# The opening in two parts of the feature columns: modulation pieces multiplied by TensorE directly, constants of its own ahead of them

## The chip, the cores and the metric

One core of one Trainium2 chip runs the whole program in one launch. The metric is the device time of the program in microseconds (us); lower is better. KB are 1,024 bytes, as in the profile.

## The reference, cut to what matters

Four layers act on one sequence of 512 tokens with 1,024 features. Each layer first needs its modulation: a vector of 1,024 conditions times a 1,024 x 3,072 matrix, split into shift, scale and gate. The first layer starts with

```python
cond = jax.nn.silu(c)
mod = cond @ ada_w[l] + ada_b[l]
shift, scale, gate = jnp.split(mod, 3, axis=-1)
h = x * (1.0 + scale[:, None, :]) + shift[:, None, :]
proj = h @ w_in
u, v, z_a, x_b, z_b = jnp.split(proj, ...)
v = layer_norm(v, norm_g, norm_b)          # per head of 256 features
sv = W_s (masked) applied to v over blocks of 128 positions, + b
a = u * sv * silu(z_a)
```

Nothing of `proj` can start before shift and scale of at least one block of 128 features are known, and for these all 1,024 rows of those matrix columns must have been read. Everything is float32 in and out.

## The kernel before, in words

The features lie across the partitions in eight blocks of 128 (`DC` = 8); `x`, `h_hi` and `h_lo` hold them as 8 x 512 tokens. For a product of full precision each operand is split into a high and a low part (`w_hi`, `w_lo`, `h_hi`, `h_lo`) and `mm3` issues three matmuls (lines 971 to 973). ScalarE makes the high parts, VectorE the low ones (`split_tile`, lines 1557 and 1883; `h_low`, line 2173, from ScalarE's `h_hi` and GpSimd's `tmp`, line 2637). Weights come as tiles of 128 x 2,048 (1,024 KB) in two turns of buffers: tile T uses the buffers of tile T - 2, so its split waits for the products of that tile.

`plan_steps` (line 88) writes out one list of steps that all engines walk through. It begins with `first_mods` and `h`, then tiles 0 to 3 (kind V, one head of 256 features each, two chunks of 256 tokens), tiles 4 to 7 (kind U), and so on. At the step `tile` T ScalarE and VectorE split tile T + 1, and VectorE sums two modulation pieces of later layers (`ada_pieces`, lines 1917 and 1925). `spatial_rows` and `spatial(h)` are TensorE's products over positions (lines 1379 and 1390) into banks 4 and 5; VectorE takes their results to `park` (line 2381). Before the change `spatial(h - 1)` stands behind the two chunks of head h. The chunks alternate between banks 0 and 1, and the first tile alone is done as a pair, block by block (`chunk_pair`, line 990), so that it can follow the blocks of `h` as they appear.

In the opening SyncE issues, in this order: the columns of constants `cols` (98.5 KB), weight tile 0, sixteen modulation pieces `ada_first` of 128 rows x 1,024 columns (512 KB each; eight of the shift, eight of the scale) with the constants `mats` and `rmats_raw` (288 and 256 KB) behind the first, then `x` in four transfers of 512 KB, weight tile 1, `ws` and `bs`. VectorE multiplies each piece by its column of `cond` and adds it to `acc` (`ada_piece`, line 1892), except pieces 1 and 3 (`DIRECT_PIECES`), which TensorE multiplies as eight one-column products each (line 1219). TensorE then sums `acc` over the partitions with a column of ones (lines 1224 and 1236), with fillers of 512 columns between (`keep_busy`, line 978), and VectorE makes `h_shift` and `h_scale` (lines 2192 and 2196). The last piece is summed in two halves, so that four blocks of the scale come out ahead.

```python
pe.wait_ge(masks_done, 1)
pe.wait_ge(upper_done, 1)
keep_busy(22)
```

Of the kernel before, what the change touches and what calls it, by code (L numbers as in the profile page):

```python
# [25 lines left out]
P = 128  # L26
D = 1024
# [48 lines left out]
DIRECT_PIECES = (1, 3)  # L76
# [11 lines left out]
def plan_steps():  # L88
# [8 lines left out]
    def begin(late_ada=False, late_low=False):  # L97

        T = st["T"]
        st["T"] += 1  # L100
        steps.append(dict(op="tile", T=T, late_ada=late_ada, late_low=late_low))
        return T
# [285 lines left out]
def build(nc, wt, adat, colst, matst, rmatst, xt, pos, wst, bst, poolt, decayt, rot, out):  # L388
# [11 lines left out]
    with ExitStack() as ctx:  # L400
# [186 lines left out]
        w_hi_done = sem("w_hi_done")  # L587
        w_lo_done = sem("w_lo_done")
# [3 lines left out]
        ada_first_landed = [sem(f"ada_first_landed{i}") for i in range(16)]  # L592
# [16 lines left out]
        ada_half = sem("ada_half")  # L609
# [129 lines left out]
        def pieces_summed(q):  # L739

            return q - sum(i < q for i in DIRECT_PIECES)
# [6 lines left out]
        for q in range(2 * SEC, SEC * UNITS):  # L748
            ada_in[q] = 16 * len(piece_at[q][0]) + ada_in.get(q - 2, 0)

# [80 lines left out]
        PAIRED = {d["C"] for d in kinds if (d["kind"], d.get("h"), d.get("c")) == ("V", 0, 0)}  # L831
# [65 lines left out]
        def _(sp):  # L897
            sp.dma_start(cols[:], colst).then_inc(cols_in, 16)
            sp.dma_start(w_raw[0][:], wt[0]).then_inc(w_landed[0], 16)
            for i in range(2 * SEC):  # L900
                sp.dma_start(ada_first[:, i, :], adat[i]).then_inc(ada_first_landed[i], 16)
# [3 lines left out]
            for i in range(4):  # L905
                sp.dma_start(x[:, 2 * i:2 * i + 2, :], xt[:, 2 * i:2 * i + 2, :]).then_inc(x_landed[i], 16)
            sp.dma_start(w_raw[1][:], wt[1]).then_inc(w_landed[1], 16)
# [31 lines left out]
            for T in range(NT):  # L939
# [8 lines left out]
                if T == 4:  # L948

                    sp.wait_ge(ada_done, pieces_summed(2 * SEC))  # L950
# [17 lines left out]
        def _(pe):  # L968
# [6 lines left out]
            def keep_busy(n):  # L975

                for i in range(n):
                    pe.matmul(bank[:, 3, :], upper, rmats[:].rearrange("p a b -> p (a b)"), start=True, stop=True)  # L978
# [11 lines left out]
            def chunk_pair(d):  # L990

                T, C = d["T"], d["C"]
                for c in range(2):
                    wait_taken(pe, BEFORE_IN_BANK[C + c])
                for k in range(DC):
                    wait_h(layer[0], k)
                    for c in range(2):
                        dst = bank[:, (C + c) % 2, :]
# [142 lines left out]
            def chunk(d, late=False, early=False):  # L1141
# [6 lines left out]
                if C in PAIRED:  # L1148
                    return chunk_pair(d)
                if C - 1 in PAIRED or kind in ("OUT2", "OUT3") and d["n"] < 2:  # L1150
# [62 lines left out]
            def first_mods():  # L1213

                pe.wait_ge(cond_done, 1)
                for i in DIRECT_PIECES:
                    pe.wait_ge(ada_first_landed[i], 16)
                    for j in range(DC):
                        pe.matmul(bank[:, 6, j:j + 1], ada_first[:, i, j * P:(j + 1) * P], cond[:, i:i + 1],
                                  start=i == DIRECT_PIECES[0] and j == 0, stop=False, skip_group_check=True)  # L1220
                pe.wait_ge(const_in, 16)
                pe.wait_ge(ada_done, pieces_summed(SEC))
                for j in range(DC):
                    ins = pe.matmul(bank[:, 6, j:j + 1], acc[:, 0, j * P:(j + 1) * P], ones[:, 0:1],
                                    start=False, stop=True, skip_group_check=True)
                ins.then_inc(first_full, 1)
                pe.wait_ge(masks_done, 1)
                pe.wait_ge(upper_done, 1)
                keep_busy(22)
                for half, bk in ((0, 7), (1, 4)):  # L1230
                    if half == 0:
                        pe.wait_ge(ada_half, 1)
                    else:
                        pe.wait_ge(ada_done, pieces_summed(2 * SEC))
                    for j in range(4 * half, 4 * half + 4):
                        ins = pe.matmul(bank[:, bk, j:j + 1], acc[:, 1, j * P:(j + 1) * P], ones[:, 0:1],
                                        start=True, stop=True)
                    ins.then_inc(first_full, 1)
                keep_busy(4)
# [119 lines left out]
            for d in steps:  # L1359
                op = d["op"]  # L1360
                if op == "tile":
                    pe.wait_ge(w_lo_done, d["T"] + 1)
# [9 lines left out]
                elif op == "first_mods":  # L1372
                    first_mods()
# [1424 lines left out]
```

## Time and profile before

| | |
|---|---|
| time, median of 3 runs | 1318.17 us (1317.94 to 1319.11) |
| time of the profiled execution | 1319.02 us |
| its span, first to last instruction | 1317.2 us |
| TensorE (PE) busy | 1289.7 us, 98% |
| VectorE (DVE) busy | 941.3 us, 71% |
| ScalarE (ACT) busy | 580.2 us, 44% |
| GpSimd (POOL) busy | 357.4 us, 27% |
| transferred | 155.18 MB, mean 118 GB/s |

The span is what the profiler sees of one execution; 1.8 us of the time lie outside it. Busy shares are averages over the whole span: the opening, where this change acts, is its first 3%. PE are matmuls, PEld weight loads, SPq SyncE's queue of transfers. Matmuls are pipelined, so the length of a single one is longer than the distance between two. A float32 matmul appears as two records, each with its own weight load. Times in the rows count from the start of the span.

### The profile page before, as it was taken

The page shows a single profiled execution, that of the slowest core. Times are in us where ns is not written, and L with a number is a line of the kernel's source. Part 1 is how long each engine was busy: PE and PEld are TensorE (multiplying, and loading weights), DVE is VectorE, ACT ScalarE, POOL GpSimd, SP SyncE. Part 2 cuts the span into 40 slices and gives each one's busy share as a digit, 9 for nine tenths or more (in the row PEclk, how much of TensorE's full clock was granted, in tenths as well). Part 3 has the DMA queues.
Part 4 walks back from the last instruction along what each step waited for, and adds up shares of the span by engine and source line. Part 5 has one row for each costly group of instructions (what it writes and reads, how often), then busy time and mean ns, then how long its engine had stood idle before and what let it go on. Part 6 is the DMA issues. An engine that isn't in the chain of part 4 may idle for free.

```text
span 1317.2 us, 18039 instructions
## 1 busy us (share of the span) xinstructions
PE 1289.7 (98%) x6874; PEld 1106.0 (84%) x6874; DVE 941.3 (71%) x1415; ACT 580.2 (44%) x889; POOL 357.4 (27%) x262
## 2 busy tenths in 40 slices
PE   5999999999999999999999999999999999999997
PEld 5998888778898888888888878888888988888887
DVE  7765654796777558888678888776785577776663
ACT  1422322321264347666422587653452477734441
POOL 1200210055620004655434221122115322221122
PEclk9999999999999999999999999999999999999999
DMA  9565666537725620111234311213533111212111
GB/s 376 171 199 180 187 201 193 158 117 204 234 79 153 174 87 21 41 52 51 88 122 142 112 65 64 96 53 110 154 97 115 65 64 65 95 55 75 64 64 64
DMA packets 35093, 155.18 MB, mean 118 GB/s; under 512 B 6848, under 2 KB 9024, under 8 KB 23744
## 3 DMA queue, kind: packets, MB, share of 16 engines
q1 hardware_dynamic: 35008, 154.04, 36.9%
q8 instruction: 54, 0.88, 0.3%
q14 instruction: 31, 0.25, 0.1%
HBM read 151.92 MB, written 2.10 MB: 117 GB/s over the span
## 4 chain that ended last, share of the span: by engine, by line
PE 88%; DVE 5%; issue 3%; ACT 1%; POOL 1%; DMA 1%; SPq 0%; DVEq 0%; POOLq 0%; ACTq 0%
PE bank L971 25%; PE bank L973 24%; PE bank L972 24%; PE bank L1334 2%; PE bank L1319 1%; PE bank L1338 1%; PE bank L1179 1%; DVE keep L2477 1%; PE bank L1510 1%; PE bank L1537 1%; PE bank L1535 1%; DMA ada_first<-adat 1%; PE bank L1307 1%; PE bank L1306 1%; PE bank L978 1%
## 5 line engine op out<-in xcount | busy, mean ns | idle before, releaser
L971 PE MATMUL bank<-h_lo,w_hi 128*128 128x512 f32 (+1 forms) x1064 | 407.1, 383 | 0.7 <-DVE k_both L2045 0.5
L973 PE MATMUL bank<-h_hi,w_hi 128*128 128x512 f32 (+1 forms) x1064 | 402.5, 378 | 0.0
L972 PE MATMUL bank<-h_hi,w_lo 128*128 128x512 f32 (+1 forms) x1064 | 402.2, 378 | 0.0
L1883 DVE TENSOR_TENSOR w_lo<-w_raw,w_hi 128x2048 fp32r<-128x2048 f32 (+2 forms) x91 | 207.1, 2275 | 75.6 <-ACT w_hi L1557 75.4
L971 PEld LDWEIGHTS bank<-h_lo,w_hi 128*128 128x128 f32 x1064 | 200.2, 188 | 37.6 <-issue 1.8
L973 PEld LDWEIGHTS bank<-h_hi,w_hi 128*128 128x128 f32 x1064 | 200.1, 188 | 37.7
L972 PEld LDWEIGHTS bank<-h_hi,w_lo 128*128 128x128 f32 x1064 | 200.3, 188 | 36.3 <-issue 0.2
L1557 ACT ACTIVATE w_hi<-w_raw 128x2048 fp32r<-128x2048 f32 (+2 forms) x91 | 166.7, 1832 | 89.7 <-PE bank L973 72.9
L1925 DVE SCALAR_TENSOR_TENSOR acc<-ada_raw,cond_four,acc 128x1024 f32<-128x1024 f32 x62 | 87.5, 1411 | 3.9 <-DMA ada_raw<-adat 1.0
L1685 ACT ACTIVATE tmp<-bank 128x512 f32<-128x512 f32 x48 | 28.8, 600 | 112.3 <-PE bank L973 111.1
L2477 DVE TENSOR_TENSOR_SCAN keep<-keep,rmats 128x127 f32<-128x127 f32 (+2 forms) x64 | 57.8, 942 | 1.0
L2599 POOL TENSOR_TENSOR beta<-beta,mats 128x256 f32<-128x256 f32 (+1 forms) x40 | 41.4, 1058 | 58.6 <-ACT beta L1842 58.6
L971 PE MATMUL bank<-mixc_lo,w_hi 128*128 128x512 f32 (+1 forms) x144 | 53.7, 373 | 0.0
L973 PE MATMUL bank<-mixc_hi,w_hi 128*128 128x512 f32 (+1 forms) x144 | 52.6, 365 | 0.0
L972 PE MATMUL bank<-mixc_hi,w_lo 128*128 128x512 f32 (+1 forms) x144 | 52.6, 365 | 0.0
L2578 POOL TENSOR_TENSOR sum<-sum,sqr 128x512 f32<-128x512 f32 x22 | 47.9, 2178 | 1.7
L2678 POOL TENSOR_TENSOR rope_t<-qr_f,sin 32x512 f32<-32x512 f32 x28 | 38.0, 1358 | 31.2 <-ACT qr_f L1814 28.8
L2565 POOL TENSOR_SCALAR mixa_hi<-park 128x512 fp32r<-128x512 f32 x8 | 11.9, 1491 | 124.4 <-DVE park L1999 124.4
L2565 POOL TENSOR_SCALAR mixc_hi<-sz 128x512 fp32r<-128x512 f32 x16 | 23.8, 1490 | 68.8 <-DVE sz L2292 68.8
L2624 POOL TENSOR_TENSOR mixf<-o_sum,ag 128x512 f32<-128x512 f32 x8 | 10.4, 1299 | 114.6 <-DVE o_sum L2532 114.6
L2577 POOL TENSOR_TENSOR sqr<-x 128x512 f32<-128x512 f32 x22 | 34.5, 1569 | 14.3 <-DVE x L2036 13.1
L2565 POOL TENSOR_SCALAR mixb_hi<-park 128x512 fp32r<-128x512 f32 x6 | 12.0, 2026 | 92.9 <-PE bank L973 92.9
(359 smaller groups left out, 2688.1 us busy)
## 6 DMA issues: line engine op xcount, KB each, us to landing
w_raw<-wt SPq DMA_DIRECT2D x83, 1024.0 KB, 5.5
ada_raw<-adat SPq DMA_DIRECT2D x256, 128.0 KB, 2.9
ada_first<-adat SPq DMA_DIRECT2D x16, 512.0 KB, 12.2
ada_raw<-adat SPq DMA_DIRECT2D x32, 256.0 KB, 5.7
w_raw<-wt SPq DMA_DIRECT2D x8, 640.0 KB, 3.9
spare_raw<-wt SPq DMA_DIRECT2D x3, 1024.0 KB, 5.1
x<-xt SPq DMA_DIRECT2D x4, 512.0 KB, 15.5
out<-outf SPq DMA_DIRECT2D x16, 128.0 KB, 1.8
```

The lines of the kernel that those rows point to most:

```text
L971: pe.matmul(dst, ah, bl, start=start, stop=False, skip_group_check=True)
L972: pe.matmul(dst, al, bh, start=False, stop=False, skip_group_check=True)
L973: return pe.matmul(dst, ah, bh, start=False, stop=stop, skip_group_check=True)
L1557: act.activation(w_hi[wb[T]][:, 0:n], w_raw[wb[T]][:, 0:n], ACT.Copy).then_inc(w_hi_done, 1)
L1883: dve.tensor_tensor(w_lo[wb[T]][:, 0:n], w_raw[wb[T]][:, 0:n], f(w_hi[wb[T]][:, 0:n]), ALU.subtract).then_inc(w_lo_done, 1)
L1925: dve.scalar_tensor_tensor(acc[:, g % 2, :], src, c, acc[:, g % 2, :], ALU.mult, ALU.add).then_inc(ada_done, 1)
L2477: ins = dve.tensor_tensor_scan(k, k, floor, 1.0, ALU.mult, ALU.max)
L2565: return pool.tensor_scalar(dst, src, 1.0, None, ALU.mult)
L2577: link(pool.tensor_tensor(sqr[:], x[:, n, :], x[:, n, :], ALU.mult))
L2578: ins = pool.tensor_tensor(sum2[:], sum2[:], sqr[:], ALU.add)
L2599: pool.tensor_tensor(blocks, blocks, strict.unsqueeze(1).broadcast_to([P, len(at), P]), ALU.mult).then_inc(seen_done, 1)
L2678: pool.tensor_tensor(rope_t[to, :], qr_f[of, :], sin1[of, :], ALU.mult).then_inc(qr_turned, 1)
```

## The change

The matrix columns of the opening are loaded and used in two parts: part 0 is feature blocks 0 to 4 (640 columns), part 1 blocks 5 to 7 (384 columns). Weight tiles 0 and 1 are loaded and split in the same parts. Modulation pieces come two in a transfer. In part 0, shift and scale, and in part 1 of the shift, every second piece (1, 3, 5, 7) is multiplied by TensorE directly; in part 1 of the scale VectorE sums all eight. TensorE starts with ten products of 197 columns of `cols`, as soon as these have landed, and puts one such product (shift) or two fillers (scale) behind each direct piece. After part 0 it works through blocks 0 to 4 of tiles 0 and 1 (`first_blocks`), with the direct pieces and sums of part 1 in between, then through blocks 5 to 7 of both. Tiles 0 and 1 so need four banks: the V chunks use banks 0 to 3. The splits of tiles 3 and 4 and the `spatial` steps move later in the list; `spatial(0)` stands behind tile 2, `spatial(1)` behind tile 3, `spatial(2)` and `spatial(3)` in tiles 4 and 5.

```diff
-DIRECT_PIECES = (1, 3)
+DIRECT_PIECES = {(0, 0): (1, 3, 5, 7), (0, 1): (1, 3, 5, 7), (1, 0): (1, 3, 5, 7), (1, 1): ()}
+FIRST_BLOCKS = 5
+X_PARTS = ((0, 2), (2, 4), (4, 5), (5, 8))
...
-    steps.append(dict(op="h", l=0))
-
-    for h in range(GH):
-        T = begin()
-        chunk("V", T, h=h, c=0)
-        chunk("V", T, h=h, c=1)
-        if h == 0:
-            steps.append(dict(op="spatial_rows"))
-        else:
-            steps.append(dict(op="spatial", h=h - 1))
-        after_tile(T)
+    steps.append(dict(op="h", l=0, part=0))
+    steps.append(dict(op="first_blocks"))
+    steps.append(dict(op="h", l=0, part=1))
+    both = [begin(split=False), begin()]
+    head_pair(0, both[0])
+    split_ahead(3)
+    steps.append(dict(op="spatial_rows"))
+    head_pair(1, both[1])
+    T = begin(split=False)
+    chunk("V", T, h=2, c=0)
+    split_ahead(4)
+    chunk("V", T, h=2, c=1)
+    spatial(0)
+    after_tile(T)
+    T = begin(split=False)
+    head_pair(3, T)
+    spatial(1)
+    after_tile(T)
...
-            if kind == "U" and i == 0:
-                steps.insert(len(steps) - 1, dict(op="spatial", h=GH - 1))
+                if kind == "U" and (i, sub) in ((0, 1), (1, 0)):
+                    spatial(2 + i)
...
+            elif d["kind"] == "V":
+                bk = 2 * (d["h"] % 2) + d["c"]
...
+            weights(0, 0)
+            for i in range(SEC):
+                ada_pair(i, 0)
                 if i == 0:
                     sp.dma_start(mats[:], matst).then_inc(const_in, 16)
                     sp.dma_start(rmats_raw[:], rmatst).then_inc(rmats_in, 16)
...
+            for i in range(3):
+                features(i)
+            weights(1, 0)
+            for i in range(SEC // 2):
+                ada_pair(i, 1)
+            weights(0, 1)
+            features(3)
+            for i in range(SEC // 2, SEC):
+                ada_pair(i, 1)
+            weights(1, 1)
...
             def first_mods():
 
+                pe.wait_ge(cols_in, 16)
+                warm_up(10)
                 pe.wait_ge(cond_done, 1)
...
+                for u in range(2):
+                    for k in DIRECT_PIECES[0, u]:
+                        direct_piece(0, u, k)
+                        if u == 1 and k == 1:
+                            pe.wait_ge(masks_done, 1)
+                            pe.wait_ge(upper_done, 1)
+                        if u == 1:
+                            keep_busy(2, 3)
+                        else:
+                            warm_up(1)
+                    if u == 0:
+                        pe.wait_ge(const_in, 16)
+                    first_sums(0, u, 6 + u)
+                keep_busy(5, 3)
+
+            def warm_up(n):
+
+                for i in range(n):
+                    pe.matmul(bank[:, 3, 0:NCOL], cols[:, 0:P], cols[:], start=True, stop=True)
+
+            def direct_piece(part, u, k):
+
+                pe.wait_ge(ada_first_landed[(SEC * u + k) // 2][part], 16)
+                for j in FIRST_K[part]:
+                    pe.matmul(bank[:, 6 + u, j:j + 1], ada_first[:, SEC * u + k, j * P:(j + 1) * P], cond[:, k:k + 1],
+                              start=k == 1 and j == FIRST_K[part][0], stop=False, skip_group_check=True)
...
+            def first_blocks():
+
+                pe.wait_ge(first_lo, 1)
+                chunk_pair(PAIRED[0], FIRST_K[0])
+                pe.wait_ge(first_lo, 2)
+                for k in FIRST_K[0]:
+                    chunk_pair(PAIRED[1], (k,))
+                    for i in DIRECT_PIECES[1, 0][2 * k:2 * k + 2]:
+                        direct_piece(1, 0, i)
+                    if k == FIRST_BLOCKS - 3:
+                        first_sums(1, 0, 6)
+                    if k == FIRST_BLOCKS - 2:
+                        first_sums(1, 1, 7)
+                keep_busy(4, 5)
...
+                elif op == "h" and d["part"] == 0:
+                    first_columns(0)
+                    for k in FIRST_K[0]:
+                        h_low(k)
+                        if 1 <= k < FIRST_BLOCKS:
+                            first_piece(left + k - 1)
+                elif op == "first_blocks":
+                    split_first(1, 0, first_hi, first_lo)
+                    for i in range(left + FIRST_BLOCKS - 1, right):
+                        first_piece(i)
+                    split_first(0, 1, w_hi_done, w_lo_done)
+                    for i in range(right, len(FIRST_ORDER)):
+                        first_piece(i)
+                    first_columns(1)
+                elif op == "h" and d["part"] == 1:
+                    for k in FIRST_K[1]:
+                        h_low(k)
+                    split_first(1, 1, w_hi_done, w_lo_done)
```

`first_piece` (VectorE) is the old sum on one part's columns; `first_sums` is the old column sum over the part's blocks; `first_columns(part)` makes `h_shift` and `h_scale` of the part's blocks. On ScalarE the step `first_blocks` splits the first part of tile 1 and the second of tile 0, and the second part of tile 1 follows part 1 of `h`.

## Rows read from the trace of the kernel before

**Rows 1.** The page: TensorE's busy time, and the chain by engine.

```profile
PE 1289.7 (98%) x6874; PEld 1106.0 (84%) x6874; DVE 941.3 (71%) x1415; ACT 580.2 (44%) x889; POOL 357.4 (27%) x262
...
PE 88%; DVE 5%; issue 3%; ACT 1%; POOL 1%; DMA 1%; SPq 0%; DVEq 0%; POOLq 0%; ACTq 0%
```

**Rows 2.** Chain that ended last, opening: start us, us, what.

```profile
4.84 9.73 DMA ada_first<-adat
...
18.76 1.29 DVE acc L1925
...
20.19 3.55 PE bank L1224 x16
23.74 7.56 PE bank L978 x22
31.30 1.68 PE bank L1236 x16
32.98 1.02 PE bank L978 x4
34.00 0.10 issue
34.10 0.36 PE bank L971
```

**Rows 3.** Windows, TensorE alone: us, busy (records), granted clock, DMA share, GB/s.

```profile
34.10:45.70 11.60, 11.60 (x97) 1.00 0.42 167
```

**Rows 4.** Windows, all engines: PE, PEld, DVE, ACT, POOL, then as above.

```profile
10.00:20.00 10.00, 6.96 (x32) 6.90 (x32) 8.21 (x8) 0.00 (x0) 1.91 (x2) 1.00 1.03 410
20.00:30.00 10.00, 9.81 (x33) 8.49 (x34) 9.10 (x10) 0.00 (x0) 0.00 (x0) 1.00 1.03 410
```

**Rows 5.** Timeline of VectorE: start us, us, instruction, idle before and releaser.

```profile
14.60 5.45 DVE L1925 SCALAR_TENSOR_TENSOR acc<-ada_first,cond,acc 128x1024 f32<-128x1024 f32 x4 [1.28 <-DMA ada_first<-adat]
...
20.99 8.23 DVE L1925 SCALAR_TENSOR_TENSOR acc<-ada_first,cond,acc 128x1024 f32<-128x1024 f32 x6 [0.28 <-DMA ada_first<-adat]
29.32 1.41 DVE L1921 SCALAR_TENSOR_TENSOR acc<-ada_first,cond,acc 128x512 f32<-128x512 f32 x2
...
32.12 0.16 DVE L2196 SCALAR_TENSOR_TENSOR h_scale<-bank,cols 128x4 f32<-128x4 f32 x1 [1.31 <-PE bank L1236]
...
33.26 0.69 DVE L2173 TENSOR_TENSOR h_lo<-tmp,h_hi 128x512 fp32r<-128x512 f32 x1
34.53 0.69 DVE L2173 TENSOR_TENSOR h_lo<-tmp,h_hi 128x512 fp32r<-128x512 f32 x1 [0.58 <-POOL tmp L2637]
...
43.47 2.28 DVE L1883 TENSOR_TENSOR w_lo<-w_raw,w_hi 128x2048 fp32r<-128x2048 f32 x1
...
48.45 0.75 DVE L1981 BATCH_NORM_STATS2 v_stats<-tmp 128x6 f32<-128x256 f32 x2
...
50.70 2.16 DVE L2371 SCALAR_TENSOR_TENSOR rb<-bank,cols,bs 128x128 f32<-128x128 f32 x8
```

**Rows 6.** Timeline of ScalarE and GpSimd, in the same columns.

```profile
6.74 1.91 ACT L1557 ACTIVATE w_hi<-w_raw 128x2048 fp32r<-128x2048 f32 x1 [3.83 <-DMA w_raw<-wt]
...
8.85 2.44 POOL L2585 TENSOR_TENSOR rmats<-mats 128x128 fp32r<-128x128 f32 x1 [8.42 <-DMA mats<-matst]
9.46 0.52 ACT L1691 ACTIVATE rmats<-rmats_raw 128x384 fp32r<-128x384 f32 x1 [0.81 <-DMA rmats_raw<-rmatst]
```

**Rows 7.** Timeline of TensorE, 10 to 18 us.

```profile
10.86 6.96 PE L1219 MATMUL bank<-cond,ada_first 128*128 128x1 f32 x32 [10.86 <-DMA ada_first<-adat]
```

**Rows 8.** Windows of line 978 alone: us, PE, PEld, granted clock, DMA.

```profile
23.60:26.40 2.80, 2.80 (x7) 2.22 (x8) 1.00 1.02 407
...
29.20:31.20 2.00, 2.00 (x10) 1.40 (x8) 1.00 1.02 408
```

**Rows 9.** Chain that ended last, around the first spatial products.

```profile
58.22 1.79 PE bank L1390 x16
```

**Rows 10.** DMA issues: operands, count, KB each, us from issue to landing.

```profile
w_raw<-wt SPq DMA_DIRECT2D x83, 1024.0 KB, 5.5
...
w_raw<-wt SPq DMA_DIRECT2D x8, 640.0 KB, 3.9
```

More of the change, by code:

```diff
@@ L749, in build, with first_summed @@
             ada_in[q] = 16 * len(piece_at[q][0]) + ada_in.get(q - 2, 0)
+        FIRST_COLS = (slice(0, FIRST_BLOCKS * P), slice(FIRST_BLOCKS * P, D))
+        FIRST_WEIGHTS = (slice(0, FIRST_BLOCKS * HD), slice(FIRST_BLOCKS * HD, TILE))
+        FIRST_K = (range(FIRST_BLOCKS), range(FIRST_BLOCKS, DC))
+        FIRST_ORDER = [(part, u, k) for part in range(2) for u in range(2) for k in range(SEC)
+                       if k not in DIRECT_PIECES[part, u]]
+        def first_summed(part, u):
+            return sum((p, v) <= (part, u) for p, v, k in FIRST_ORDER)
         def wait_tile_done(eng, T):
@@ L898, in _, with weights, ada_pair, features @@
             sp.dma_start(cols[:], colst).then_inc(cols_in, 16)
-            sp.dma_start(w_raw[0][:], wt[0]).then_inc(w_landed[0], 16)
-            for i in range(2 * SEC):
-                sp.dma_start(ada_first[:, i, :], adat[i]).then_inc(ada_first_landed[i], 16)
+            def weights(T, part):
+                c = FIRST_WEIGHTS[part]
+                sp.dma_start(w_raw[T][:, c], wt[T, :, c]).then_inc((w_landed if part else first_landed)[T], 16)
+            def ada_pair(i, part):
+                c = FIRST_COLS[part]
+                i2 = slice(2 * i, 2 * i + 2)
+                sp.dma_start(ada_first[:, i2, c],
+                             adat[i2, :, c].rearrange("i p d -> p i d")).then_inc(ada_first_landed[i][part], 16)
+            def features(i):
+                k = slice(*X_PARTS[i])
+                sp.dma_start(x[:, k, :], xt[:, k, :]).then_inc(x_landed[i], 16)
+            weights(0, 0)
+            for i in range(SEC):
+                ada_pair(i, 0)
                 if i == 0:
@@ L1147, in chunk @@
                     return
-                if C in PAIRED:
-                    return chunk_pair(d)
-                if C - 1 in PAIRED or kind in ("OUT2", "OUT3") and d["n"] < 2:
+                if C == PAIRED[0]["C"]:
+                    for pair in PAIRED:
+                        pe.wait_ge(w_lo_done, pair["T"] + 1)
+                        chunk_pair(pair, FIRST_K[1])
+                if C in IN_PAIRS or kind in ("OUT2", "OUT3") and d["n"] < 2:
                     return
@@ new lines, in first_sums @@
+            def first_sums(part, u, bk):
+                pe.wait_ge(first_sum, first_summed(part, u))
+                own = not DIRECT_PIECES[part, u]
+                for j in FIRST_K[part]:
+                    ins = pe.matmul(bank[:, bk, j:j + 1], acc[:, u, j * P:(j + 1) * P], ones[:, 0:1],
+                                    start=own and j == FIRST_K[part][0], stop=True, skip_group_check=True)
+                ins.then_inc(first_full, 1)
+            def first_blocks():
[11 more added lines that the diff above has]
+                keep_busy(4, 5)
@@ L1696, in _ @@
                 if op == "tile":
-                    for T in split_with(d["T"]):
+                    for T in split_with(d["T"]) if d["split"] else ():
                         split_tile(T)
+                elif op == "split_ahead":
+                    split_tile(d["T"])
+                elif op == "first_blocks":
+                    split_first(1, 0, first_hi)
+                    split_first(0, 1, w_hi_done)
                 elif op == "chunk":
@@ L2347, in _ @@
                     T = d["T"]
-                    if not d["late_low"]:
+                    if d["split"] and not d["late_low"]:
                         for t in split_with(T):
```

155 lines of the change are left out of this document (75 added, 80 removed).

## The prediction, made before the change was built

> **What bounds the kernel now.** I read the page first. TensorE is busy for 98% of the span and carries 88% of the chain that ended last [rows 1]. So what happens in the first 34 us decides this change, and whatever TensorE wins there lasts only if it does not wait longer later.
>
> The chain of the opening came next [rows 2]. The reader is to see four links: a transfer of `ada_first` that lands at 14.57, VectorE's sums, TensorE's column products and fillers, and at 34.10 the first product of the layer. Before 34.10 TensorE does no product of the layer. From 34.10 to 45.70 it runs one tile of V (96 products of 256 columns) without a gap [rows 3], 0.12 us each, 1.45 us for the twelve of one feature block.
>
> Then the transfers. The two windows from 10 to 30 us move 410 GB/s at a DMA share of 1.03 [rows 4]: the queue is full. Counting what was issued in order, 4,226 KB had to land by 14.57 and 6,786 KB by 20.97 (VectorE waits for pieces 4 and 9) [rows 5]: 2,560 KB in 6.4 us, 2.5 us for 1,000 KB. That line gives t = 4.0 + KB x 0.0025. It also hits the first weight tile (1,122 KB: 6.8, seen 6.74), `mats` (1,922 KB: 8.8, seen 8.85) and `rmats_raw` (2,178 KB: 9.4, seen 9.46) [rows 6]. The last piece (9,858 KB) is due at 28.6. VectorE, at 1.37 us a piece, starts it at 29.3 [rows 5]: transfers and VectorE are both nearly the bound, and 5.5 us follow from 28.6 to 34.10.
>
> **The change, part by part.** (1) *Part 0 of the columns.* Five of eight blocks are 640 columns. Ahead of them lie 98.5 + 640 (first weights) + 544 (constants) KB, then eight pairs of 640 KB, 1.6 us each. By the line the pairs land at 7.4, 10.4, 12.0, 13.6, 15.2, 16.8, 18.4 and 20.0; the constants lie between the first two. 3,456 KB of the old load are simply behind: 8.6 us. SyncE's issues, 0.4 to 0.7 us each, are fewer and not the limit. Rows become 2,560 bytes; `mats` and `rmats_raw` have rows of 2,304 and 2,048 bytes and kept the line, so I charge nothing here; 1,536-byte rows of part 1 have no row.
>
> (2) *VectorE's sums* shrink from 14 pieces of 1,024 to 8 of 640 columns. An update costs 1.28 us for 1,024 and 0.70 for 512 [rows 5]; between them 0.85 for 640. One per 1.6 us pair: VectorE is done at 20.0 + 0.1 + 0.85 = 20.95 and is no bound.
>
> (3) *TensorE's direct pieces* take the rest. One column with 128x128 weights is two records. At the lower clock 32 of them took 6.96 us, 0.435 us a product; the 8 products of the later sums took 1.68 us, 0.21 [rows 2, 7]. The filler between tells the clock: 7 in 2.8 us up to 26.4 (0.40 to 0.43 for 512 columns, that is 1.2 GHz), 10 in 2.0 us after 29.2 (0.21, 2.4 GHz) [rows 8]; the column of granted clock reads 1.00 in both. So 7 us of one-column work did not lift it and 5.5 us of wide work did, and 1.7 us of one-column work after did not drop it. The new `warm_up(10)` is ten 197-column products. The spatial products, 128 columns in the same type, take 1.79/8 = 0.22 us [rows 9], so a 197-column one is 0.34, and 0.69 at half clock: ten from 2.8 us last until 6.3 to 9.7. I take the rise at about the time seen, done at 8.0 to 8.5. After that a pair costs 5 x 0.21 + 0.34 = 1.4 us in the shift and 1.05 + 0.44 = 1.5 in the scale, under the 1.6 of a pair. But the five shift sums (1.05) go between: pair 3 done 15.0, sums 16.0, then 17.5, 19.0, 20.5, 22.0, and the scale sums 23.05. TensorE ends 3 us behind the last landing and is the new bound of the opening.
>
> (4) *From the sums to the first product.* Now the first four scale columns are out at 31.98 (31.14 plus four products), `h_scale` starts at 32.12, `h_lo` at 33.26, TensorE at 34.10 [rows 2, 5]: 2.1 us. The features are on time (block pairs at 21.3 and 22.6). First product at 25.2 instead of 34.1: **8.9 us earlier**.
>
> (5) *Supply of blocks 0 to 4.* `h_lo` comes every 1.27 us [rows 5] against a need of 1.45. Four part-1 updates (0.56 us, extrapolated to 384 columns) now stand behind blocks 1 to 4 on VectorE, and their pairs land at 25.7, 26.7, 27.7 and 28.6. Each block then costs 0.69 + 0.56 and lands for TensorE by 30.2, needed at 31.0. Next `w_lo` of tile 1's first part: ScalarE is free at 27.0, weights landed 24.8, VectorE 30.8 to 32.25; TensorE asks at 25.2 + 7.2 = 32.4. The margin is 0.2 us, and what is late on VectorE is late there.
>
> (6) *Added to TensorE's real stretch*: 12 direct products and 6 sums at 0.21 = 3.8 us, `keep_busy(4, 5)` 0.9 (hides the step below): **4.7 us back**. Tile 1's part ends 32.4 + 7.2 + 3.8 = 43.4, fillers 44.3. The scale sums stand before the last block at 41.3; their last pair lands at 35.3 and VectorE's eight updates end by 38. `first_full` 4 at 41.95, plus 2.0 gives block 5 at 44.0: hidden by the fillers and one block; without them the wait would be the same time. Then 3 + 3 blocks end both tiles at 52.9, and the row sums (0.9) at 53.8. Before, the same work ends at 58.2 [rows 9]. **Gain so far 4.4 us.**
>
> (7) *What queues up behind.* Splits of tiles 2 to 4 and the four V posts now come in a lump. Tile 2 waits for tile 0's end at 48.6: ScalarE 1.9 and VectorE 2.3 us (1.91 and 2.28 seen [rows 5, 6]) give 52.9, needed 53.8. From there VectorE is behind: a V post takes 2.25 us and `rb` 2.2 [rows 5]. Two posts 57.4, tile 3's `w_lo` waits for ScalarE's root, then 61.2, `rb` 63.4, two posts 68.1, two pieces 70.3, V(2,0) 72.5, tile 4's `w_lo` 76.1, V(2,1) 78.4, `spatial(0)`'s two results 79.1 and 79.8. `spatial(1)` on TensorE now stands after tile 3, at 78.6, and needs those banks back: **0.55 us lost**. Tiles 3, 4 and 5 ask at 67.1, 80.9 and 93.7, margins 6, 5 and 3 us. On SyncE the load of tile 3 now waits for `w_lo` of tile 1's second part, at 48.1 instead of 45.75 [rows 5]; it lands some 5.5 us later [rows 10], at 53.6, and ScalarE, held by its roots, does not come to it before 57. Behind it stand the piece loads and the `poolw` load, which wait for VectorE's first updates of group 2, as they do now; tile 5's weights, behind those, land near 78 and are split from 86 on. If this cover were absent, each microsecond of VectorE past 79 would be one of TensorE.
>
> Sum: 8.9 - 4.7 + 0.2 (the old stretch from 34.1 to 58.2 holds 0.2 us of change-overs that 0.12 us a product does not count, and I count none in the new one) - 0.55 = 3.85 us. The profiled execution took 1319.02 (span 1317.2 and 1.8 around it); less 3.85 is 1315.2. The median is 0.85 under that execution, so **1314.3**. A no-change band is 0.2%, 2.6 us.
>
> **A rule against it.** The Trainium skill, DMA: Bandwidth & Descriptors, section Measured (under Bandwidth), says to batch transfers to at least 1 MiB for 75% of peak or more, measured there with GpSimd's queue; the change cuts 1,024 KB to 640 and 384. The rows speak against it: 256 KB and 288 KB transfers in the full queue cost only their bytes [rows 4, 6].
>
> **Rivals.** *A. The clock falls again while pairs are awaited* (ends slower). Only 0.34 to 0.44 us of a 1.6 us pair is wide work, and the row shows that one-column work alone never lifted it [rows 7]. Then a shift pair costs 2.2 + 0.69 = 2.9 and a scale pair 3.05: from 9.5 the sums end at 9.5 + 11.6 + 2.2 + 12.2 + 2.2 = 37.7, first product 39.8, and about 2.7 us more until the clock rises: 5.7 + 2.7 + 4.7 = 13 later, 1331. If only the shift half is slow, the scale half from 23.3 ends at 30.4, first product 32.5: 1.6 - 4.7 - 0.5 = 3.6 later, 1322. The gain is gone when TensorE's sums end after about 27. For it: those duties; against: no idle stretch over 1.3 us. Chance 0.16.
>
> *B. The lump costs more.* GpSimd's `tmp` sets the 1.27 us period, and with VectorE fuller it may be 1.6; `w_lo` of tile 1 misses by 1 us, and `spatial(1)` waits 1 more. Gain 1.2 to 2.6: 1315.6 to 1317. Chance 0.19.
>
> *C. The queue loses rate with small transfers.* One 640 KB load alone takes 3.9 us, against 5.5 for 1,024 KB [rows 10]: 0.71 of the time for 0.62 of the bytes, an excess that overlap hides today. If it did not, 6,402 KB would take 15% more, 2.4 us; TensorE's lag absorbs none. Gain 1.4, 1316.8. At three quarters of the rate the last pair lands 5.3 us later and the gain is gone: 1319.6. That is also what the rule of the Trainium skill's page, DMA: Bandwidth & Descriptors, would make of it. Chance 0.04 in all.
>
> *D. As worked out*, 1312.6 to 1315.6 (the direct pieces may run closer to the landings, up to 1 us more gain; tile 1's margin may cost 1). Chance 0.61.
>
> **Numbers.** The low end allows TensorE to be 1 us behind the landings instead of 3: 1312.0. The high end takes in B, C and the milder half of A: 1320.5; above lies about 0.12. Faster: D and a little of B, 0.62. Same: most of B and C, 0.20. Slower: A and a rest, 0.18.
>
> **What would show it.** One-column records at 0.105 us spacing from about 10 us on (A: 0.217); VectorE's last part-0 update ending near 21; first product of 256 columns near 25.2; no gap before tile 1's first product near 32.4; first product of block 5 near 44.3; tile 2's first near 53.8; a wait of about half a microsecond before `spatial(1)`. The prediction fails if the clock drops, or if TensorE waits for `w_lo` or `h_lo` by microseconds between 25 and 80.

## The result, and the profile after

The changed kernel takes 1329.20 us (median of 6 runs, 1328.46 to 1330.92) against 1318.78 for the kernel before (6 runs, 1317.94 to 1320.94): a ratio of 1.008, 95% interval 1.0067 to 1.0093. It is 10.4 us slower, where 1314.3 and faster was forecast. The profiled execution took 1328.74, its span 1326.9. (One of the 19 executions of the kernel before that were run beside x1_vector to x4_bare was in a slow state, 4592.67 us, and counts in no ratio.)

Page of the changed kernel, the lines of the clock and of the chain by engine (40 slices of 33 us):

```profile
PEclk6899999999999999999999999999999999999998
...
PE 88%; DVE 5%; issue 3%; ACT 1%; POOL 1%; DMA 1%; SPq 0%; DVEq 0%; POOLq 0%; ACTq 0%
```

The chain is shared out as before [rows 1]. The clock is not: the first slice has 6 tenths and the second 8. From the third on both kernels read 9, but for the last, 8 instead of 9. Windows of TensorE in the changed kernel (us, busy with records, granted clock, DMA share, GB/s):

```profile
9.30:10.90 1.60, 0.31 (x2) 1.00 1.04 414
12.00:12.60 0.60, 0.60 (x5) 1.00 1.03 393
12.60:13.00 0.40, 0.40 (x3) 0.71 1.04 397
13.00:14.00 1.00, 1.00 (x6) 0.50 1.05 402
39.00:40.00 1.00, 1.00 (x7) 0.50 0.05 20
40.00:41.00 1.00, 1.00 (x10) 0.96 0.00 0
```

The clock fell at about 12.8 us, from 2.4 to 1.2 GHz, and came back at 40.1. Ahead of the fall TensorE had waited 1.4 us for the second pair, and then done five one-column products and one of 197 columns. The chain of the same stretch, with what the low clock did to it:

```profile
10.99 1.28 PE bank L1302 x10
...
20.45 2.13 PE bank L1302 x10
22.58 1.06 PE bank L1038 x2
...
32.61 1.93 PE bank L1310 x10
34.53 2.34 PE bank L1038 x5
36.87 0.23 PE bank L1031
...
46.97 1.23 PE bank L1302 x12
...
66.56 0.86 PE bank L1470 x2
78.92 1.79 PE bank L1481 x16
92.22 1.79 PE bank L1481 x16
```

Line 1302 are the direct products, 1310 the one-column sums, 1038 the fillers, 1031 the first of a block's products, 1470 the row sums, 1481 `spatial`. Five direct products (ten records) take 2.13 us where 1.05 was forecast, two fillers 1.06 instead of 0.44. The group at 10.99, ahead of the fall, took 1.28. The sums end at 34.5 and the first product starts at 36.87 (34.10 before [rows 2]); the chain lets a product start where the one ahead ends, and the timeline, from which the table below is taken, has 36.67.

VectorE in the changed kernel, its timeline:

```profile
10.97 0.89 DVE L2012 SCALAR_TENSOR_TENSOR acc<-ada_first,cond,acc 128x640 f32<-128x640 f32 x1 [1.48 <-DMA ada_first<-adat]
12.63 0.89 DVE L2012 SCALAR_TENSOR_TENSOR acc<-ada_first,cond,acc 128x640 f32<-128x640 f32 x1 [0.78 <-DMA ada_first<-adat]
...
20.91 0.88 DVE L2012 SCALAR_TENSOR_TENSOR acc<-ada_first,cond,acc 128x640 f32<-128x640 f32 x1 [0.77 <-DMA ada_first<-adat]
21.71 0.16 DVE L2304 TENSOR_TENSOR h_shift<-bank,cols 128x5 f32<-128x5 f32 x1
34.57 0.17 DVE L2306 SCALAR_TENSOR_TENSOR h_scale<-bank,cols 128x5 f32<-128x5 f32 x1 [12.70 <-PE bank L1310]
35.71 0.69 DVE L2283 TENSOR_TENSOR h_lo<-tmp,h_hi 128x512 fp32r<-128x512 f32 x1 [0.98 <-POOL tmp L2764]
```

This is the plainest picture of the loss: the last pair is there at 20.9 and VectorE's last update ends at 21.8, but `h_scale` waits 12.7 us for TensorE. Before, the same wait was 1.3 us [rows 5]. The transfers kept nearly their rate: pairs of 640 KB came every 1.66 us, 396 GB/s, against 410 [rows 4].

**Where the 9.2 us up to tile 2 went.** Tile 2's first product starts at 67.42 (66.56 + 0.86); before it is 58.2 without its spatial step [rows 9]. Of this the first product is 2.8 later (36.87 for 34.10, by the chain). The stretch from there to tile 2 takes 30.55 instead of 24.1 us: 1.45 for 16 products at half rate, 3.6 for the 18 one-column products (two groups of 1.23, two of 0.56), 0.93 for the fillers ahead of block 5, and 0.5 that is mostly the slower first product behind each change of type. The spans differ by 9.7. The starts of VectorE's `w_lo` show where the other half microsecond lies: they differ by 9.2 us at 465 us of the kernel before (473.88 for 464.65), by 9.45 at 651 (660.69 for 651.24) and at 1286 (1295.37 for 1285.90), and a last quarter comes behind that. Its cause is not known.

### The profile page after: what moved, and what is told of

Read it like the earlier page. It is cut to its first block, busy times and chain, and to the rows that moved or that the text cites. A ratio compares the mean times of both kernels' runs of the same rounds, so it can differ in the third digit from the quotient of the medians.

```text
span 1326.9 us, 18239 instructions
## 1 busy us (share of the span) xinstructions
PE 1308.4 (99%) x6965; PEld 1123.8 (85%) x6965; DVE 939.6 (71%) x1423; ACT 580.0 (44%) x891; POOL 356.1 (27%) x262
## 4 chain that ended last, share of the span: by engine, by line
PE 88%; DVE 5%; issue 3%; ACT 1%; POOL 1%; DMA 1%; SPq 0%; DVEq 0%; POOLq 0%; ACTq 0%
PE bank L1031 25%; PE bank L1033 24%; PE bank L1032 24%; PE bank L1422 2%; PE bank L1407 1%; PE bank L1302 1%; PE bank L1426 1%; PE bank L1239 1%; DVE keep L2604 1%; PE bank L1601 1%; PE bank L1628 1%; PE bank L1626 1%; PE bank L1395 1%; PE bank L1394 1%; PE bank L1443 1%
## 5 line engine op out<-in xcount | busy, mean ns | idle before, releaser
L1987 DVE TENSOR_TENSOR w_lo<-w_raw,w_hi 128x2048 fp32r<-128x2048 f32 (+2 forms) x89 | 202.2, 2272 | 77.0 <-ACT w_hi L1648 76.8
L1648 ACT ACTIVATE w_hi<-w_raw 128x2048 fp32r<-128x2048 f32 (+2 forms) x89 | 162.9, 1831 | 89.8 <-PE bank L1033 86.5
L2726 POOL TENSOR_TENSOR beta<-beta,mats 128x256 f32<-128x256 f32 (+1 forms) x40 | 41.4, 1058 | 58.6 <-ACT beta L1946 58.6
L2751 POOL TENSOR_TENSOR mixf<-o_sum,ag 128x512 f32<-128x512 f32 x8 | 10.4, 1299 | 114.5 <-DVE o_sum L2659 114.5
L2704 POOL TENSOR_TENSOR sqr<-x 128x512 f32<-128x512 f32 x22 | 36.5, 1657 | 14.2 <-DVE x L2146 13.1
L1031 PE MATMUL bank<-w_lo,h_hi 128*128 128x256 f32 x128 | 37.9, 296 | 0.0
## 6 DMA issues: line engine op xcount, KB each, us to landing
ada_first<-adat SPq DMA_DIRECT2D x8, 640.0 KB, 10.4
```

Of the source, the lines that this page charges most:

```text
L1031: pe.matmul(dst, ah, bl, start=start, stop=False, skip_group_check=True)
L1648: act.activation(w_hi[wb[T]][:, 0:n], w_raw[wb[T]][:, 0:n], ACT.Copy).then_inc(w_hi_done, 1)
L1987: dve.tensor_tensor(w_lo[wb[T]][:, 0:n], w_raw[wb[T]][:, 0:n], f(w_hi[wb[T]][:, 0:n]), ALU.subtract).then_inc(w_lo_done, 1)
L2704: link(pool.tensor_tensor(sqr[:], x[:, n, :], x[:, n, :], ALU.mult))
L2726: pool.tensor_tensor(blocks, blocks, strict.unsqueeze(1).broadcast_to([P, len(at), P]), ALU.mult).then_inc(seen_done, 1)
```

## The experiments

The milestones in one table. "First product" is the first 256-column product, "tile 2" the end of the row sums (for the kernel before and the one without fillers, the start of `spatial(0)`, which there comes ahead of tile 2); "clock low" is where the windows of the opening show less than 1.00 behind the first rise or, where none is shown, where the distance of the products tells it. Times of the first three columns are of the profiled execution, as its timeline has them. Medians are of 4 executions for x3_dense, x4_bare and v3_scale_direct and of 10 to 12 for the other experiments. The profiled execution is the fastest of four for x3_dense and the slowest of eleven for v1_guard and v2_best.

| kernel | first product | tile 2 | clock low in the opening | median us | before beside it | ratio (95%) |
|---|---|---|---|---|---|---|
| before | 34.10 | 58.2 | up between 26.4 and 29.2 [rows 8] | 1318.78 | | |
| changed | 36.67 | 67.4 | 12.8 to 40.1 | 1329.20 | 1318.78 | 1.0080 (1.0067, 1.0093) |
| x2_last | 26.98 | 57.5 | 26.4 to 29.8 | 1320.00 | 1319.17 | 1.0004 (0.9995, 1.0014) |
| x1_vector | 27.72 | 57.4 | none | 1319.53 | 1319.17 | 0.9998 (0.9988, 1.0007) |
| x3_dense | 33.38 | 63.1 | 20.7 to 34.4 | 1326.88 | 1319.17 | 1.0060 (1.0043, 1.0077) |
| x4_bare | 33.05 | 62.9 | never up before 34 | 1327.36 | 1319.17 | 1.0062 (1.0047, 1.0077) |
| y2_part1 | 28.77 | 59.2 | 17.7 to 24.5, 48 to 52 | 1321.32 | 1319.02 | 1.0018 (1.0009, 1.0027) |
| y1_three | 29.79 | 59.5 | 17 to 24, 27 to 31 | 1322.72 | 1319.02 | 1.0021 (1.0010, 1.0033) |
| z2_vector_part1 | 28.85 | 58.4 | 19.3 to 22.7 | 1320.79 | 1319.02 | 1.0011 (1.0001, 1.0021) |
| z1_cold_before | 35.42 | 61.3 | up only at 39.5 | 1321.85 | 1319.02 | 1.0023 (1.0014, 1.0032) |
| v1_guard | 29.68 | 59.4 | none | 1321.03 | 1319.26 | 1.0015 (1.0006, 1.0024) |
| v2_best | 29.30 | 58.6 | none | 1320.22 | 1319.26 | 1.0007 (0.9998, 1.0016) |
| v3_scale_direct | 33.20 | 64.0 | 19.6 to 36.7 | 1325.73 | 1319.26 | 1.0049 (1.0036, 1.0063) |

Theory A is that the clock fell because TensorE's wide work was sparse, and that the direct products then ran behind the transfers. Theory B is that the parted opening costs the time by itself.

**x2_last and x1_vector: take the direct pieces away.**

```diff
-DIRECT_PIECES = {(0, 0): (1, 3, 5, 7), (0, 1): (1, 3, 5, 7), ...}
+DIRECT_PIECES = {(0, 0): (7,), (0, 1): (7,), ...}          # x2_last
+DIRECT_PIECES = {(0, 0): (), (0, 1): (), ...}              # x1_vector
...
-                warm_up(10)
+                warm_up(29)                                # x1_vector: 35
...
+                keep_busy(20, 3)                           # x1_vector: 24
```

> Only piece 7 of shift and of scale is multiplied by TensorE in part 0; VectorE sums the other fourteen, and TensorE runs wide fillers without a break (29 products of 197 columns, later 20 of 512). Theory A (the clock falls at 12.7 us because wide work is sparse, and the one-column products at half rate then run behind the transfers): the clock stays up from about 6.5 us, the scale sums end near 23.0, first product near 25.2 instead of 36.87, and 1.4 us of half-rate products go too: about 13 us under the changed kernel, 1316, and 2 to 3 us under the kernel before. Theory B (the parts themselves cost the time: the part-1 products and sums in the first blocks and the lump of VectorE's work, with the opening hidden by the transfers anyway): no more than 3 us under the changed kernel, 1326 or more.

> No direct piece in part 0: VectorE sums all sixteen, TensorE runs fillers (35 of 197 columns, 24 of 512). Theory A: as the run with piece 7 direct, but VectorE ends its last two updates at 22.7 instead of 21.8, so the first product comes near 26.0: 1317. Theory B: 1326 or more.

Windows of x1_vector, TensorE:

```profile
15.00:20.00 5.00, 5.00 (x32) 1.00 1.04 399
20.00:25.00 5.00, 4.54 (x23) 1.00 1.02 400
25.00:30.00 5.00, 4.24 (x31) 1.00 1.08 389
```

And its VectorE, timeline:

```profile
17.55 6.82 DVE L2004 SCALAR_TENSOR_TENSOR acc<-ada_first,cond,acc 128x640 f32<-128x640 f32 x7
...
25.74 0.16 DVE L2298 SCALAR_TENSOR_TENSOR h_scale<-bank,cols 128x5 f32<-128x5 f32 x1 [1.29 <-PE bank L1302]
...
33.21 0.61 DVE L2004 SCALAR_TENSOR_TENSOR acc<-ada_first,cond,acc 128x384 f32<-128x384 f32 x1
33.73 2.35 DVE L1992 TENSOR_TENSOR w_lo<-w_raw,w_hi 128x1280 fp32r<-128x1280 f32 x2
```

The wait for TensorE is back at 1.29 us and the first product at 27.72, 9 us before the changed kernel's. The medians are 9.2 and 9.7 us under it. Theory B allowed 3; A is right on the size of this step. But 13 and 12 us were expected, and the kernel before is not beaten. The reader sees why in the fence: seven updates of 640 columns take 6.82 us, 0.98 each (0.89 and the wait for the one before it), so VectorE, with two per pair of 1.66 us, ends at 24.4 instead of 22.7. In the blocks it needs 1.57 us for each pair of `h_lo` and update, and the first of the two `w_lo`, tile 1's, ends at 35.2; TensorE starts its last product of tile 0's part at 34.87 and the next at 35.27, 0.3 us later than without a wait. x2_last wins 0.7 at the first product and loses it again: its clock falls at 26.4, while TensorE waits for the first block.

A second reason lies in the executions. In x1_vector's profiled one the clock held, tile 2 came 0.8 us ahead of the kernel before and the span is 0.9 us shorter (1316.3 for 1317.2). Its ten executions go with their mean granted clock: the three with 0.998 took 1317.9 to 1318.1 us, the two with 0.995 and 0.994 took 1320.2 and 1321.9. The kernel before does the same, 1318.0 to 1319.4 at 0.998 and 1321.9 at 0.994. So by the trace the parted opening with all of part 0 on VectorE gains about 0.8 us where the clock holds, which so few executions do not prove, and the median loses it again.

**x3_dense, x4_bare and v3_scale_direct: grade the filling.**

```diff
-                            keep_busy(2, 3)
+                            keep_busy(3, 3)                # x3_dense
...
-                            warm_up(1)
+                            warm_up(6 if k == 1 else 2)    # x3_dense
```

```diff
-                warm_up(10)
...
-                        if u == 1:
-                            keep_busy(2, 3)
-                        else:
-                            warm_up(1)                     # all gone in x4_bare
```

```diff
-DIRECT_PIECES = {(0, 0): (1, 3, 5, 7), (0, 1): (1, 3, 5, 7), ...}
+DIRECT_PIECES = {(0, 0): (), (0, 1): (1, 3, 5, 7), ...}    # v3_scale_direct, with 37 warm-up products
```

> The changed kernel with its eight direct pieces, but more wide work between: 6 instead of 1 product of 197 columns behind the first shift piece, 2 behind the others, 3 instead of 2 fillers behind each scale piece. Theory A: if this is enough to hold the clock, scale sums end near 25 and the first product comes at 27.3: 1318 to 1319. If it is not enough, the added fillers at half rate only lengthen the chain, first product near 43, 1336. Theory B: the opening is hidden, so within 2 us of the changed kernel, 1329.

> The changed kernel without its warm-up products and without the fillers between the direct pieces (the five fillers ahead of the first blocks stay). Theory A: the one-column products never raise the clock; at 0.435 us each the scale sums end near 30.6, first product near 32.9, about 4 us before the changed kernel's: 1325, still slower than the kernel before. Theory B: within 2 us of the changed kernel.

> Only the shift half of the changed kernel's direct pieces is undone (VectorE sums it, 37 products of 197 columns run meanwhile); the scale half keeps its four direct pieces with two fillers behind each. Theory A: the clock is up at 17 us and falls in the scale half, between 20 and 22; the rest of the pieces and the sums at half rate put the first product near 31, between the changed kernel's 36.9 and the 27.7 of the run without direct pieces: 1323 to 1325. If the shift half alone was the trouble: first product near 27.6, 1319.

Windows of TensorE in x3_dense, where the clock falls:

```profile
20.00:21.00 1.00, 1.00 (x10) 0.86 1.02 398
21.00:22.00 1.00, 1.00 (x3) 0.50 1.03 412
```

In v3_scale_direct:

```profile
16.00:18.00 2.00, 1.94 (x15) 1.00 1.03 393
18.00:20.00 2.00, 2.00 (x16) 0.91 1.05 402
20.00:22.00 2.00, 2.00 (x12) 0.50 1.03 405
```

And the timeline of TensorE in x4_bare:

```profile
20.10 8.67 PE L1297 MATMUL bank<-cond,ada_first 128*128 128x1 f32 x40
28.63 2.27 PE L1305 MATMUL bank<-mats,acc 128*128 128x1 f32 x10
30.77 2.48 PE L1038 MATMUL bank<-rmats 128*128 128x512 f32 x5
33.05 0.43 PE L1031 MATMUL bank<-w_lo,h_hi 128*128 128x256 f32 x1
```

x3_dense met none of its cases. The filling carried the clock through the whole shift half, past the 12.8 us of the changed kernel, and lost it at 20.7, in the scale half. TensorE had had no gap since its first warm-up product, so the fall followed no wait. Its median is 2.3 us under the changed kernel; the other three executions show a lower mean clock (0.989 to 0.991) than the profiled one (0.993), so in them it was low for longer. v3_scale_direct says the same from the other side: with 14 us of dense wide work in front and no direct piece in the shift, the clock fell at 19.6, 1.5 us after the scale half's pieces began, and the first product came at 33.2 (31 expected). x4_bare ran every one-column product at 0.43 us and yet had its first product 3.6 us before the changed kernel's (4 expected): at the low clock the fillers were pure cost. Its median is only 1.8 under the changed kernel's where 4 were expected. In the profiled execution tile 2 is 4.5 us earlier, and 5.1 us were lost again later, in two further falls of the clock (under v1_guard and in the last section).

**z1_cold_before: the price of a low clock in the kernel before.**

```diff
-                keep_busy(22)
```

> The kernel before without its 22 fillers ahead of the scale sums. Theory A: the clock is still low at the sums and at the first products; the sums are about as early, the four fillers behind them end at 35.3 instead of 34.0, and about 3.7 us of products run at half rate: 3 us slower than the kernel before, 1322. Theory B (the clock of the opening costs nothing that the transfers do not hide): no difference.

2.8 us slower (interval 1.8 to 4.2), with `spatial(0)` at 61.33 instead of 58.22. The row is

```profile
61.33 1.79 PE bank L1389 x16
```

TensorE's products run at half rate until 39.5 there (0.21 us each, then 0.12). So in the kernel before the 22 fillers, with VectorE's sums running meanwhile, are worth 3 us, and the change took that order apart.

**y1_three, y2_part1 and z2_vector_part1: other divisions of the work.**

```diff
-DIRECT_PIECES = {(0, 0): (1, 3, 5, 7), (0, 1): (1, 3, 5, 7), (1, 0): (1, 3, 5, 7), (1, 1): ()}
+DIRECT_PIECES = {(0, 0): (7,), (0, 1): (3, 7), (1, 0): (1, 3, 5, 7), (1, 1): ()}   # y1_three
+DIRECT_PIECES = {(0, 0): (7,), (0, 1): (3, 7), (1, 0): (7,), (1, 1): ()}           # y2_part1
+DIRECT_PIECES = {(0, 0): (), (0, 1): (), (1, 0): (), (1, 1): ()}                   # z2_vector_part1
...
-                    if k == FIRST_BLOCKS - 2:
+                    if k == FIRST_BLOCKS - 1:              # y2_part1, z2_vector_part1
                         first_sums(1, 1, 7)
```

y1_three and y2_part1 also start with 29 warm-up products, and have 2 and 10 fillers between the pieces of the scale and ten ahead of the first blocks; z2_vector_part1 has x1_vector's opening.

> The same opening (three direct pieces in part 0, fillers between, ten ahead of the first blocks), with part 1 as in the changed kernel. First product near 25.8, tile 2 near 55.2: 1317.3. If the clock falls between 22 and 26 as in the run with piece 7 alone, 1.5 us more: 1319.

> Direct pieces only where VectorE cannot keep up (piece 7 of the shift, 3 and 7 of the scale, in part 1 piece 7 of the shift alone), wide fillers everywhere between, ten ahead of the first blocks, and the scale sums of part 1 behind the last block instead of before it. Theory A (clock) with the prices read so far: first product near 25.8, nine one-column products of part 1 fewer (1.9 us and two change-overs), part 1 of the scale then waits on VectorE; tile 2 starts near 53.8 instead of 57.4: 3.6 us under the run in which VectorE sums all: 1316, 3 us under the kernel before. Theory B2 (after the clock, VectorE's updates at 1.0 us each and its part-1 work bound the opening, whatever TensorE does): tile 2 not before 56.5, 1318.5 or more.

> The run in which VectorE sums all of part 0, with part 1 of the shift summed by VectorE too and the last scale sums behind the last block. If TensorE's extra products are what the first blocks lose (3.0 us with their change-overs), tile 2 comes 3 us earlier, at 54.4. If VectorE's sixteen updates take their place, its last one ends near 44.6, block 5 is ready near 47.2 and tile 2 starts at 57.0: 0.4 us gained, 1319.

All three missed the better case expected of them, by 2 to 5 us, and in all three the clock fell in the opening. Windows of z2_vector_part1, whose TensorE has the same program as x1_vector's up to 30 us:

```profile
16.00:18.00 2.00, 0.72 (x7) 1.00 1.03 393
18.00:20.00 2.00, 2.00 (x11) 0.83 1.05 401
20.00:22.00 2.00, 2.00 (x6) 0.50 1.04 406
```

In one execution of this opening the clock stays up, in another it falls behind the shift sums. The timelines of TensorE show a difference between the two, x1_vector first:

```profile
2.69 14.56 PE L1288 MATMUL bank<-cols 128*128 128x197 f32 x70 [2.69 <-DMA cols<-colst]
17.13 1.25 PE L1302 MATMUL bank<-mats,acc 128*128 128x1 f32 x10
...
2.78 13.34 PE L1288 MATMUL bank<-cols 128*128 128x197 f32 x70 [2.78 <-DMA cols<-colst]
17.39 1.25 PE L1302 MATMUL bank<-mats,acc 128*128 128x1 f32 x10 [1.28 <-DVE acc L2004]
```

In z2_vector_part1 the 35 warm-up products took 1.2 us less, and TensorE then waited 1.28 us for the shift sums; in x1_vector it did not wait. That goes with the fall but does not prove its cause: x2_last waited 1.15 us at 14.2 and its clock held until 26.4. The medians of these kernels mix executions of both kinds. Their runs spread over 5 to 8 us, and go with the mean granted clock: y1_three took 1318.1 us at 0.995 and 1326.2 at 0.988, z2_vector_part1 1318.2 at 0.998 and 1323.7 at 0.991.

What z2 was meant to show holds beside it: without the twelve direct products of part 1 TensorE waits 0.8 us for VectorE's sums and 1.5 for `h_lo`, and the stretch from the first product to tile 2 is as long as x1_vector's (29.6 and 29.7 us), so the product time was handed to VectorE, not saved. In y2_part1 too TensorE waits 1.5 us for `h_lo`, at 48, and there its clock falls a second time; its theory B2, by which VectorE's part-1 work sets the time, is not refuted.

**v1_guard and v2_best: hold the clock, then pay the other debts.**

```diff
+                warm_up(37)
...
+                first_sums(0, 0, 6, 1)      # a filler between any two one-column sums
+                keep_busy(24, 3)
+                first_sums(0, 1, 7, 1)
+                keep_busy(9, 3)
...
-                        if 1 <= k < FIRST_BLOCKS:
+                        if 1 <= k < 3:      # v2_best: w_lo of tile 1 ahead of two updates
...
-                keep_busy(4, 5)             # v2_best
```

> VectorE sums all of part 0 and TensorE never leaves wide work for long: 37 products of 197 columns until the shift sums are due, a 512-column filler between any two one-column sums, 24 between the two sets, nine ahead of the first blocks. Theory A: no fall of the clock before tile 2. The four fillers inside the scale sums cost 0.9 us: first product near 28.6, tile 2 near 58.3, as the kernel before with its one spatial step set apart (58.2): 1319, and a narrower spread than the 5 to 8 us of the runs whose clock fell at 16 to 19 us. Theory C (the parted opening has a loss of its own beside the clock): tile 2 after 59, 1321 as in the last runs.

> The same, and the low part of tile 1's weights is made ahead of two of the four part-1 updates (0.8 us of waiting gone), and the four fillers behind the first blocks are left out (0.5 us, since block 5 is ready 0.4 us after TensorE gets there). Tile 2 near 57.0: 1317.8, 1.2 us under the kernel before, less than the 0.2% that can be told. If the clock is what it hangs on, it must not fall before tile 2.

Windows of v1_guard:

```profile
2.80:40.00 37.20, 37.08 (x219) 1.00 1.01 371
...
740.00:745.00 5.00, 4.83 (x32) 0.75 0.17 21
745.00:750.00 5.00, 5.00 (x26) 0.50 0.96 385
750.00:755.00 5.00, 5.00 (x34) 0.73 0.79 331
```

The opening now runs without a fall in both, as A said. Tile 2 starts at 59.4 (58.3 expected) and 58.6 (57.0 expected), against 58.2 before: the first product is 4.4 to 4.8 us earlier than in the kernel before, and the stretch to tile 2 is 29.3 to 29.7 us instead of 24.1. That settles what theory B is worth: with the clock held in this way, by fillers that put the first product 1.6 to 2.0 us behind x1_vector's, the parted opening gives back all that it wins; without them 0.8 us stay. The 0.9 us of the four fillers that v2_best leaves out come back there as a wait of 1.0 for `h_lo` of block 5.

The spread is 3.9 and 4.1 us, narrower than the 8 of y1_three and like that of the kernel before beside them (3.8). The lower rows show a part of it. Near 740 us, in the border behind the second layer, TensorE again has one-column sums among half-width products. There the clock fell for some 10 us in these two profiled executions, which are the slowest of their eleven (mean clock 0.994; 0.996 to 0.998 in most others), so the medians hold little of it. Compared with x1_vector's, v1_guard's span is 5.6 us longer and its tile 2 only 2.0 later. The other 3.6 lie there: VectorE's `w_lo` starts 1.94 us later than x1_vector's at 728 (730.40 for 728.46) and 5.54 later at 766 (771.87 for 766.33).

## Why the prediction was wrong, step by step

**The step that failed** is part (3): "I take the rise at about the time seen, done at 8.0 to 8.5. After that a pair costs ... 1.4 us in the shift and 1.05 + 0.44 = 1.5 in the scale, under the 1.6 of a pair." The rise came as said; records of line 1296 in windows of the changed kernel:

```profile
2.70:4.50 1.80, 1.79 (x5) 1.79 (x6) 1.00 0.88 299
...
6.50:7.90 1.40, 1.38 (x9) 1.08 (x7) 1.00 0.97 312
```

But it did not last: from 12.8 on a pair cost 2.8 to 3.0 us in the shift and 3.0 to 3.2 in the scale, and TensorE's sums ended at 34.5 instead of 23.05. This was rival A, at a chance of 0.16, with its prices right (2.9 and 3.05) and its end (1331) 2 us off; its end is nearer than its parts, since it had the clock low from 9.5 on and the first product at 39.8. The row that should have moved the chances was named in the text: 7 us of one-column work at the low clock without a rise [rows 7]. I set against it that 1.7 us of such work behind the 22 fillers had not dropped the clock [rows 2], and that is a stretch far shorter than the change's. I also set against it that no idle stretch would exceed 1.3 us; the one ahead of the fall was 1.4, and x3_dense fell without one.

**Parts (1) and (2), transfers and VectorE's updates**: mechanism right, sizes off. The last pair was due at 20.0 and is taken at 20.91: the second already came at 10.97 for 10.4, and then a pair took 1.66 us for 1.6. An update of 640 columns takes 0.89 us and 0.98 in a row, for 0.85. The Trainium skill, DMA: Bandwidth & Descriptors, section Measured (under Bandwidth), asks for 1 MiB and more for 75% of peak or more. The trace disagrees for this queue: 640 KB transfers kept 97% of the rate that [rows 4] show.

**Part (4)**, 2.1 us from the sums to the first product: 2.3 (34.53 to 36.87), with a low clock. **Part (5)**: `h_lo` and update took 1.57 us a block instead of 1.25. The mis-sized term is the update of 384 columns: 1.05 us between two `h_lo`, where 0.56 was charged; the one behind the last `h_lo` took 0.61 (33.21 in x1_vector's fence). Where the clock was up TensorE lost 0.3 us before tile 1 to `w_lo` (x1_vector), which the margin of 0.2 had announced. In the changed kernel the low clock of the first blocks hid it.

**Part (6)**, 4.7 us back: measured 3.6 + 0.9, and 0.5 of change-overs that I had not counted. **Part (7)**, the lump on VectorE: right in order, wrong by 0.5 us to the careful side. `spatial(1)` found its banks free at 92.2, just as tile 3 ended, and waited for nothing.

**The range** was not drawn from its own working. The high end, 1320.5, was said to take in the milder half of A, but the prediction works that half out as 1322.

**What the likeliest case would have been worth.** Its first product was due at 25.2 and tile 2 at 53.8. With the sizes as measured, the direct pieces at full rate would end at 22.8, the sums at 24.0, the first product would start at 26.3, and 29.7 us more (x1_vector's stretch) give 56.0: a gain of 2.2 us. That is an estimate, since no kernel with eight direct pieces in part 0 held its clock. So even without the fall the forecast of a clear gain rested on 2.2 us of prices set too low.

**What stays open**: that the clock fell, and what it cost, is read from the records; that sparse wide work made it fall is the best account, not shown by itself. With direct pieces in both halves or in the scale alone it fell and stayed low for 13.7 us or more (changed, x3_dense, v3_scale_direct), without them in part 0 it held (x1_vector, v1_guard, v2_best) or fell for 3.4 us (z2_vector_part1). Open are also what decides that the same opening holds the clock in one execution and not in another (x1_vector and z2_vector_part1), why an update of 384 columns takes 1.05 us between two `h_lo`, and the half microsecond behind tile 2. No version beat the kernel before by its median; x1_vector, x2_last and v2_best equal it.

## What to carry to other kernels

Work moved to an idle TensorE has to be priced at both clocks. One-column products fill its time, and here did nothing for its clock: in x4_bare 19 us of them without a gap (11.5 to 30.8) did not raise it. A chain that fits between transfers only at the full one is a risk, not a gain. When a stage is begun earlier by splitting it, count what the split adds to the stage behind it: here 4.4 to 6.4 us of earlier start (v1_guard, v2_best, x1_vector) bought 5.2 to 5.6 us of longer blocks. And look at whether the engine that gets the time next (VectorE, at 0.98 us an update) has it to give.

## What the runs showed of the hardware that was not expected

- The granted clock fell while TensorE was busy without a gap, or nearly (0.06 us idle between 16 and 18 us in v3_scale_direct): at 20.7 us in x3_dense and at 19.6 in v3_scale_direct, in each case among five-product groups of one column with fillers between. The Trainium skill, TensorE: Matmul & The Clock Gate, section HAM oscillation, tells of falls through long waits for transfers between bursts of products. The traces here go beyond that: the clock fell behind a wait of 1.4 us in the changed kernel, and behind none to speak of in these two.
- The column of granted clock reads 1.00 from the start of the span though the clock is at 1.2 GHz: ten records of x4_bare took 2.27 us at a reading of 1.00, and the fillers of [rows 8] likewise. In these traces it agreed with the distance of the products from the first fall on, not before.
- The clock falls in the middle of the kernel too, in some executions: near 366 us (x2_last, x4_bare, y2_part1, z1_cold_before) and near 745 (x4_bare, v1_guard, v2_best). By the starts of `w_lo` on either side, set against x1_vector's, which has neither fall, the first costs 1.5 us (x2_last: 0.1 behind at 356, 1.6 at 389) and the second 3.6. A change of a few microseconds is measured through this: the medians here follow the times of tile 2 only within 3.5 us, while in each single trace tile 2 and these two prices give the span to within half a microsecond.
